# Sliding-window attention on the full matmul array with zero-padded keys, and the squares of two norms added up before their column sums

## The reference, cut to what matters

```python
yg = yg.reshape(b, s, SSM_GROUPS, SSM_INNER // SSM_GROUPS)          # 2 groups of 512
yg = yg * lax.rsqrt(jnp.mean(yg * yg, axis=-1, keepdims=True) + RMS_EPS)
...
mem_kv = _rmsnorm(mem, norm_mem) @ w_mem_kv                         # mem: 256 x 1024
...
def _sliding_window_branch(q, k, v, z, sinks):                      # 128 positions a block
    ...                                                             # q: 2 kv heads x 4 x 64
    s = jnp.einsum("bnqkgd,bnskd->bnkgqs", q, kb) * (SW_HD ** -0.5) # SW_HD = 64
    s = jnp.where(valid[None, :, None, None], s, NEG_INF)           # window of 128
    p = jax.nn.softmax(jnp.concatenate([s, sink], axis=-1), axis=-1)[..., :-1]
    o = jnp.einsum("bnkgqs,bnskd->bnqkgd", p, vb).reshape(B, T, BRANCH_W)
    return o * jax.nn.silu(z)
```

## Time and profile before

| | |
|---|---|
| median of 3 runs | 880.71 us (880.54 to 880.88) |
| the profiled execution: its own time | 881.82 us |
| its span in the trace | 880.0 us |
| granted TensorE clock, mean | 0.995 of full speed |
| busy: TensorE, its weight loads, VectorE, ScalarE, GpSimd | 859.8, 780.8, 623.1, 509.1, 73.6 us |
| chain that ended last | TensorE 89%, VectorE 5%, ScalarE 3% |

### The profile page before, as it was taken

One profiled execution on the slowest core, in us unless ns is written; L12 is line 12 of the kernel. 1 busy time (PEld: TensorE's weight loads), 2 busy tenths in 40 slices (PEclk: granted clock), 3 DMA queues, 4 the chain that ended last, 5 costly groups with the idle time before them and its releaser, 6 DMA issues.

```text
span 880.0 us, 14646 instructions
## 1 busy us (share of the span) xinstructions
PE 859.8 (98%) x5816; PEld 780.8 (89%) x5816; DVE 623.1 (71%) x1124; ACT 509.1 (58%) x826; POOL 73.6 (8%) x76
## 2 busy tenths in 40 slices
PE   6999999999999999999999999999999999999997
PEld 6999999999989999999998799999999776778885
DVE  6787987988867766666656787787456455775765
ACT  5565777665377656656657688544444434454443
POOL 0200002001020211111113000500000000000000
PEclk9999999999999999999999999999999999999999
DMA  9457443457455655555564555643322322365541
GB/s 344 146 194 276 159 145 108 169 179 291 140 186 174 239 190 175 187 191 175 185 198 137 181 188 201 222 145 124 117 97 96 113 104 96 119 205 195 197 146 48
DMA packets 40588, 149.21 MB, mean 170 GB/s; under 512 B 4524, under 2 KB 4680, under 8 KB 39880
## 3 DMA queue, kind: packets, MB, share of 16 engines
q1 hardware_dynamic: 40520, 148.27, 49.3%
HBM read 147.18 MB, written 1.08 MB: 168 GB/s over the span
## 4 chain that ended last, share of the span: by engine, by line
PE 89%; DVE 5%; ACT 3%; issue 1%; DMA 1%; SPq 0%; DVEq 0%; ACTq 0%
PE bank L610 40%; PE bank L605 16%; PE bank L606 16%; PE bank L607 16%; PE bank L613 2%; DVE t_wl L1739 2%; DVE t_arena L1744 1%; DVE t_arena L1754 1%; DVE t_x L1754 1%; ACT t_hh L1237 1%; DMA t_x<-in_xin 1%; DVE t_sm L1751 1%; ACT t_arena L1237 1%; ACT t_wh L1232 0%; ACT t_br L1237 0%
## 5 line engine op out<-in xcount | busy, mean ns | idle before, releaser
L1739 DVE TENSOR_TENSOR t_wl<-t_raw,t_wh 128x1024 fp32r<-128x1024 f32 x260 | 316.5, 1226 | 114.3 <-ACT t_wh L1232 113.4
L1232 ACT ACTIVATE t_wh<-t_raw 128x1024 fp32r<-128x1024 f32 x260 | 273.4, 1058 | 129.1 <-PE bank L610 60.3
L605 PE MATMUL bank<-t_hh,t_wh 128*128 128x256 f32 x1144 | 330.3, 289 | 2.2 <-DVE t_hl L1744 1.5
L607 PE MATMUL bank<-t_hh,t_wl 128*128 128x256 f32 x1144 | 323.6, 283 | 0.0
L606 PE MATMUL bank<-t_hl,t_wh 128*128 128x256 f32 x1144 | 323.5, 283 | 0.0
L605 PEld LDWEIGHTS bank<-t_hh,t_wh 128*128 128x128 f32 x1144 | 219.1, 192 | 6.1 <-issue 4.2
L606 PEld LDWEIGHTS bank<-t_hl,t_wh 128*128 128x128 f32 x1144 | 219.2, 192 | 0.8
L607 PEld LDWEIGHTS bank<-t_hh,t_wl 128*128 128x128 f32 x1144 | 219.1, 192 | 0.0
L610 PE MATMUL bank<-t_wh,t_br 128*128 128x512 f32 x384 | 123.8, 393 | 0.2 <-POOL t_br L2448 0.2
L1754 DVE SCALAR_TENSOR_TENSOR t_arena<-bank,t_par,t_arena 128x255 f32<-128x255 f32 (+2 forms) x184 | 75.3, 474 | 45.0 <-ACT t_arena L1237 44.7
L610 PE MATMUL bank<-t_wh,t_hh 128*128 128x512 f32 x224 | 92.0, 411 | 1.8 <-DVE t_wl L1739 1.8
(11 more groups left out here) (152 smaller groups left out, 840.3 us busy)
## 6 DMA issues: line engine op xcount, KB each, us to landing
t_raw<-in_ws SPq DMA_DIRECT2D x260, 512.0 KB, 3.9
t_br<-decay SPq DMA_DIRECT2D x1, 2048.0 KB, 8.3
t_arena<-in_post SPq DMA_DIRECT2D x3, 512.0 KB, 5.5
t_arena<-gates SPq DMA_DIRECT2D x1, 1536.0 KB, 10.5
t_x<-in_xin SPq DMA_DIRECT2D x4, 256.0 KB, 5.5
t_bd<-in_bd SPq DMA_DIRECT2D x1, 1024.0 KB, 11.7
t_x<-in_xtok SPq DMA_DIRECT2D x1, 1024.0 KB, 5.8
t_arena<-in_mem SPq DMA_DIRECT2D x1, 1024.0 KB, 8.0
```

What stands on the lines that cost most here:

```text
L605: e.matmul(o, wh, xh, start=first, stop=False, skip_group_check=True)
L607: return e.matmul(o, wl, xh, start=False, stop=last, skip_group_check=True)
L1232: e.activation(WH[q % NS][:, :], RAW[q % NR][:, :], ACT.Copy, bias=0.0, scale=1.0).then_inc(*hi.now(q))
L1739: e.tensor_tensor(WL[q % NS][:, :], RAW[q % NR][:, :], WH[q % NS][:, :].bitcast(F), SUB).then_inc(*lo.now(q))
```

## The change

`SWK_` (one tile, both key heads) becomes `SWK2` (two tiles): tile `a` has key head `a` on its own 64 partitions and zeros on the others. The score products then take all 128 rows of a query tile and of `SWK2[:, a]`; the value products take all 128 columns of `SWV_` as weights and write all 128 partitions of bank 6, of which the next step reads 64 as before. GpSimd writes the zeros once (memset of 128x512 at tick 166), and ScalarE waits for it and copies the keys in two pieces of 64x256. In both norms VectorE adds the squares down to one tile for each sum, by one more add for each of the mixer's two groups and two more for `mem`, and TensorE sums one tile each.

```diff
-        SWQt, SWK_ = ar(12, 4, T), ar(16, 1, T)
+        SWQt, SWK2 = ar(12, 4, T), ar(58, 2, T)
...
+            def mem_sums():
+                e.wait_ge(*d_add.of("mem", 3))
+                column_sums(3, 0, [MEMQ[:, 0, :]], True, True).then_inc(*p_norm.now("mem", "sum"))
...
-                    m = column_sums(3, 2 * g, [SSQ[:, 4 * g + k, :] for k in range(2)], g == 0, g == 1)
+                    m = column_sums(3, 2 * g, [SSQ[:, 4 * g, :]], g == 0, g == 1)
...
-                    r = slice(64 * a_, 64 * a_ + 64)
-                    kt, q = SWK_[r, 0, :], SWQt[r, i, :]
+                    kt, q = SWK2[:, a_, :], SWQt[:, i, :]
...
-                    o = PB[6][r, :]
-                    mm(o[:, 0:T], SWV_[:, 0, r], pt[:, 0:T], True, False)
-                    mm(o[:, 128:T], SWV_[:, 1, r], pt[:, T:384], False, True).then_inc(*p_sw.now("o", i, a_))
+                    mm(PB[6][:, 0:T], SWV_[:, 0, :], pt[:, 0:T], True, False)
+                    mm(PB[6][:, 128:T], SWV_[:, 1, :], pt[:, T:384], False, True).then_inc(*p_sw.now("o", i, a_))
...
-            norm_sums_first("mem", 3, MEMQ)
-            norm_sums_last("mem", 3, MEMQ)
+            mem_sums()
...
-            act(SWK_[:, 0, :], half(BANK["swkv"], 0), ACT.Copy)
+            e.wait_ge(*g_dn.of("pads"))
+            for a in range(2):
+                act(SWK2[64 * a:64 * a + 64, a, :], half(BANK["swkv"], 0)[64 * a:64 * a + 64, :], ACT.Copy)
...
-                       ADD).then_inc(*d_ssd.now("gsum", g))
+                       ADD).then_inc(*d_ssd.now("gsums", g))
+                    e.wait_ge(*d_ssd.of("gsums", g))
+                    tt(SSQ[:, 4 * g, :], SSQ[:, 4 * g, :], SSQ[:, 4 * g + 1, :], ADD).then_inc(*d_ssd.now("gsum", g))
...
             square_adds("mem", MEMQ)
+            e.wait_ge(*a_sq.of("mem", 3))
+            e.wait_ge(*d_add.of("mem", 1))
+            tt(MEMQ[:, 0:2, :], MEMQ[:, 0:2, :], MEMQ[:, 6:8, :], ADD).then_inc(*d_add.now("mem", 2))
+            e.wait_ge(*d_add.of("mem", 2))
+            tt(MEMQ[:, 0, :], MEMQ[:, 0, :], MEMQ[:, 1, :], ADD).then_inc(*d_add.now("mem", 3))
...
+                        e.memset(SWK2, 0.0).then_inc(*g_dn.now("pads"))
```

## The result

The changed kernel takes 873.7 us (median of 4 runs, 872.87 to 874.92), the kernel before, on the same chip, 880.62 (880.42 to 880.88). The ratio is 0.9919, 95% interval 0.9906 to 0.9932. The forecast was 873.9. The profiled execution took 873.42 us with a span of 871.6; before it was 881.82 with 880.0.

A forecast was written before the change was run, and what follows sets the result against it. TensorE's queue was taken as the bound (98% busy). Attention -5.1 us, column sums -2.2 and a longer wait +0.45 summed to -6.8, taking the median from 880.7 to 873.9 us, range 873.2 to 874.8 (71%).

The forecast's parts named there:

- The bound: Whole kernel: TensorE's queue sets the time, busy 98% of 880.0 us; edits gain what leaves it, less later waits.
- Value groups, 2.55 us: Attention: full 128*128 shape saves 0.34 us in each of seven value groups and 0.17 in the fourth.
- Score groups, 3.12 us: Attention: full shape saves 0.39 us (0.33 to 0.45) in each of eight score groups.
- Given back at the turn, 0.58 us: DeltaNet output turn at 755.17: 0.58 us of the attention gain becomes a wait for VectorE's scaling.
- Column sums, 2.2 us: Mixer and `mem` norms: 20 TensorE passes removed at 0.11 us each, 2.2 us.
- the adds' 0.45: Mixer norm: VectorE's new group 0 add lengthens TensorE's wait before `pl0` by 0.45 us.
- an estimate from the figure in the Trainium skill: Rival on both norms' column sums: 0.025 us a pass, sums give only 0.5 us, time 875.6; 1%.
- The adds of `mem`, the memset, the copies: 0: VectorE's `mem` adds, GpSimd's zeros and ScalarE's third copy finish before TensorE needs them: cost 0.
- the excess is not the shape's: Rival, attention groups: excess is the price of short groups; only column sums count, 878.9 us; 7%.
- the zeros come late: Rival, near 597.56 us: key copies wait for GpSimd's memset, delaying weight splits; slower, above 882 if after about 612; 2%.
- half shapes are the cheap ones: Rival, attention's 16 groups: half-array passes cost half, so widening doubles their 0.66 us; 884.5 us; 1%.
- the rule of row tiling: Attention: skill says row-tile contractions of 64 for up to twice the speed; forecast limited it to tiles side by side.

The follow-up runs named there:

- Experiment 4: Kernel before with only the value groups widened to 128 weight columns; score groups keep 64 rows, column sums as before: 879.19 us (ratio 0.9974).
- Experiment 3: Kernel before with only the score groups on the full 128 rows; value groups keep 64 columns, column sums as before: 878.15 us (ratio 0.9961).
- experiment 1: Kernel before with the attention part only (padded keys, full-width values), both norms' sums as before: 876.29 us (ratio 0.9938).
- experiment 2: Kernel before with the shortened column sums only, attention's score and value groups cut to 64 again: 879.26 us (ratio 0.9973).
- experiments 6: Changed kernel with the first head of each pair's value products using 96 of the 128 weight columns: 872.53 us (one run).
- 9: Changed kernel with each head's value product split into two 64-column halves of the same 128 columns, one after the other: 876.98 us (one run).
- experiment 8: Changed kernel with full-width products also in the mixer's eight state-space pairs, VectorE reading each pair by two instructions: 878.41 us (ratio 0.9961).
- experiment 10: Changed kernel with two heads' value products back to back in 64-column tiles, the first head's turned weights held in their own buffer: 871.78 us (ratio 0.9893).
- two small moves: Changed kernel with VectorE's first mixer norm adds at tick 51 (was 49) and TensorE's DeltaNet turn at tick 210 (was 209): 872.49 us (ratio 0.99).
- the last kernel: Experiment 12: changed kernel with norm adds at tick 51, DeltaNet turn at tick 210 and two heads' value products side by side: 870.5 us (ratio 0.9877).

## Why the prediction was right

- *The bound.* Right. About 8.0 us were taken out of TensorE's queue (2.24 of column sums, 2.58 and 3.14 of groups), 7.0 came off, and the difference is the two waits that the forecast had named (0.46 and 0.55).
- *Value groups, 2.55 us.* Experiment 4 has 2.58: seven groups by 0.33 to 0.37 and the fourth, where half was taken, by 0.13.
- *Score groups, 3.12 us.* Experiment 3 has 3.14 for the eight. The mask product with no change of shape behind it was priced by columns at 0.17 and takes 0.18. The forecast had left 0.33 to 0.45 us a group open here; it is 0.39 to 0.40.
- *Given back at the turn, 0.58 us.* Right in place and cause: 0.55 of the starts' gain is lost between 752 and 758 us, 0.34 of it from the scores and 0.19 from the values (0.39 and 0.2 in the forecast). No other wait of TensorE grew between 600 and 792 us. Attention in all: 5.1 forecast, 5.2 measured (experiment 1).
- *Column sums, 2.2 us, and the adds' 0.45.* 0.09 to 0.11 us a pass and 0.46 us more at `pl0`. Net 1.75 forecast, 1.77 measured (experiment 2). By an estimate from the figure in the Trainium skill ("TensorEngine Tiling (Array Packing)", Instruction Overhead) the sums would have given 1.7 us less; the trace of the changed kernel decides against it, 0.81 us for eight passes.
- *The adds of `mem`, the memset, the copies: 0.* Right for the adds and the copies; the dependent adds took 2.66 us where 2.5 was worked out. For the memset it is in part luck. The forecast looked only at whether the zeros come in time. In four of the thirteen kernels that have the memset TensorE lost 0.4 to 0.6 us between 497 and 600 us, in a chain of VectorE that stretches beside GpSimd's instructions (last section). The changed kernel's profiled run was not among them.
- *Rivals.* That the excess is not the shape's is excluded by experiments 6 and 9: 96 columns in a full tile cost nothing more, and 64 in a half tile cost 0.34 with the same work. That the zeros come late: the memset is done at 547.81 us, some 46 us before the copies. That half shapes are the cheap ones: false as priced (a pass doesn't get shorter) but true in another way, which experiments 8 to 10 show. The sentence on the rule of row tiling in the forecast ("holds only where two tiles run side by side") was argued there from the groups' distance. Now it is shown for column tiles: side by side the half shape wins by 0.30 us a pair. For the row tiles of the scores it wasn't tried.
- *What the forecast missed.* The granted clock's changes from one execution to the next. The forecast for the profiled execution was 875.0, worked out from before's 881.82, which had two pieces of 3.4 us at 1.2 GHz; it took 873.42. Of the 1.6 us between them 1.5 are this luck, not the change. The median came out at 873.7 for 873.9.

## What to carry to other kernels

An isolated product on half of the array between full-shape products costs about 0.35 us for going there and back, and no time is saved by its smaller size; widen it with zeros or with a neighbour's operand if the other half has nothing to do. If two such products can be issued back to back on different column halves, keep the half shape: the second is free, and widening them loses 0.3 us a pair. For row halves no run here shows it. When you shorten TensorE's queue, look up which instruction now stands too early in it: two small moves brought back 1.2 us here.

## What was not expected of the hardware

**The clock's pieces.** From one execution to the next TensorE's granted clock may or may not fall to 1.2 GHz for 3.4 us near 15 us and near 489 us. In experiment 8 a piece stood at 194.8 us instead, and the one at 14.6 us in the last kernel was 6.8 us long. The time of the first rise differs too, from 11.2 to 15.0 us over the fourteen traces. In the trace of before the engine was busy for 3.82 of the 4 us from 9 to 13 (at 1.2 GHz up to 11.4) and for 2.25 of the 4 from 484 to 488, ahead of its two pieces; in the changed kernel's trace it was busy for 4.00 (all at 1.2 GHz) and 2.51, and no piece followed. The variant with attention only was busy for 2.25 from 484 to 488 as well, and none followed there either. What decides it, the traces don't show. That it is a matter of executions and not of kernels, the kernel before shows, which ran many times: the three runs with a mean granted clock of 0.999 took 879.75 to 880.48 us, the eleven with 0.995 took 881.78 to 882.62. It is worth 1 to 3 us in a run, more than most single terms of this change, so edits of less than 1 us were read from the stretches and not from the times.

**VectorE's small ops stretch beside GpSimd's.** In the kernel with the pairs (experiment 10) the norm chain near 547 us has an op of 0.59 us which took 0.17 in the changed kernel. VectorE and GpSimd, the kernel with pairs:

```profile
547.08 0.59 DVE L1762 TENSOR_SCALAR t_sm<-t_sm 128x8 int32<-128x8 int32 x1
...
550.74 0.97 DVE L1755 TENSOR_TENSOR t_sm<-t_sm 128x8 f32<-128x8 f32 x3
...
547.12 0.53 POOL L2508 MEMSET t_arena<- 128x512 f32 x1 [68.72 <-DMA t_arena<-gates]
...
550.81 0.88 POOL L2468 TENSOR_TENSOR t_arena<-t_arena,t_maskD 128x128 f32<-128x128 f32 x2
```

The long ones end with GpSimd's: 547.67 and 547.65, 551.71 and 551.69. The same ops in the changed kernel, where GpSimd's fall 0.1 to 0.2 us differently against them (its long one is the next behind 547.16, of 0.47 us):

```profile
547.16 0.17 DVE L1754 TENSOR_SCALAR t_sm<-t_sm 128x8 int32<-128x8 int32 x1
...
550.71 0.35 DVE L1747 TENSOR_TENSOR t_sm<-t_sm 128x8 f32<-128x8 f32 x3
```

The chain from 546.6 on takes 5.15 us with the pairs and 4.42 in the changed kernel, and with the pairs TensorE waits 0.42 us for it near 552.2. All fourteen traces agree with this: each op of the chain that takes 0.38 us or more ends 0.02 to 0.03 us behind an op of GpSimd. The chain takes 3.85 to 5.15 us, and TensorE waits in just the four where it takes 5.0 or more (experiments 1, 8, 10 and 12). In the kernel before, which has no memset, it takes 3.95. That VectorE's ops wait there for GpSimd's is what the ends suggest; no experiment took GpSimd's away, so it stays a reading, and how much of it is the memset's is open.
